# RWKV's low-rank inputs taken from the input and its difference, and attention run as one sequence of 32 units

## The chip, the cores and the metric

The kernel runs on one core of a Trainium2 chip. A core has five engines that each work through a queue of their own in order: TensorE (PE, with its weight loads as PEld), VectorE (DVE), ScalarE (ACT), GpSimd (POOL) and SyncE (SP), which here issues the weight DMAs. The metric is the time of one execution on the device in microseconds (us); lower is better.

## The reference

Four layers are computed for T = 512 positions of width D = 1024, in fp32: a convolution mixer, an RWKV-7 mixer, a gated delta rule mixer and a "stick breaking" attention, each with an MLP. The change touches two places. In the RWKV mixer, six inputs are mixed from the normed input h and its difference to the position before:

```python
xx = h_prev - h
xr, xw, xk, xv, xa, xg = h[None] + xx[None] * mu[:, None, None, :]
r, k, v = jnp.einsum('nbsd,nde->nbse', jnp.stack([xr, xk, xv]), w_rkv)
w = -jax.nn.softplus(-(w0 + jnp.tanh(xw @ w1) @ w2)) - 0.5
a = jax.nn.sigmoid(a0 + (xa @ a1) @ a2)
g = jax.nn.sigmoid(xg @ g1) @ g2
```

`w1` and `a1` are 1024x64, `g1` is 1024x160. In the attention (8 heads of 128), for each block of queries:

```python
z = jnp.einsum('bhtd,bhsd->bhts', qb, kb) * scale
ls_neg = jax.nn.log_sigmoid(-z)
log_fail = jnp.where(causal, ls_neg, 0.0)
log_rest = lax.cumsum(log_fail, axis=3, reverse=True) - log_fail
log_a = z + ls_neg + log_rest
att = jnp.where(causal, jnp.exp(log_a), 0.0)
outs.append(jnp.einsum('bhts,bhsd->bhtd', att, vb))
```

## The kernel before, in words

Activations lie transposed in SBUF, as 8 tiles (k = 0 to 7) of 128 features x 512 positions. A large matrix product is made in three parts for accuracy: the input is split into a rounded part HH (ACT, `scalar_split`, L627) and a remainder HL (DVE, L1101 here), the weights likewise into WH (ACT, L401) and WL (DVE, L409), and PE adds WH·HH, WL·HH and WH·HL (L650, L651, L656). Weights stream in as chunks through three buffers ST by SP; `plan_take`, `scalar_take` and `vector_take` place the conversion of a later chunk in the queue of an engine while an earlier one is used. A projection of 1024x1024 ("rkv" chunks 0 to 11, four for each of r, k and v) is 192 matmuls, four chunks of 48. Engines wait on counters ("tallies"); the order in each queue is the order in which the functions below write it.

**RWKV projections (us 610 to 827 of the trace).** After the rms norm, DVE scales X into TMP (L1121), ACT adds the shift and writes HT (L1074), POOL subtracts the shifted HT and writes the difference VV (L1143). TMP has two buffers. Then six mixes follow in the order W, A, G, r, k, v: DVE writes TMP = VV·mu + HT (L1107), ACT splits off HH (L627), DVE writes HL (L1101), 8 of each a mix. There is one HH and one HL, so ACT may write the next mix's HH only when the product that reads the last one has ended: that is the wait `mm.at(*free)` in `scalar_split`. The low-rank products (L1044, `tensor_lora`) are four runs of 24 matmuls: W, A, and twice G (G's 160 columns in two windows). The last ones are followed by r, k and v.

**Attention (us 2592 to 2716).** Heads 0 to 3 go together, then 4 to 7. For a head, the key blocks j = 3, 2, 1, 0 are taken in turn, each with w = 512 - 128j queries; so j = 0 is the widest. For each (head, j):

- PE "z": scores, one product of width w (L2664); ACT: ZS, abs, exp, ln, each of width w (L2704, L2707, L2709, L2711)
- DVE "softplus" (L2733, width w), "fail" and "masked" (L2736, L2737, width 128)
- PE "rest": the sums over later keys, products of width w, w - 128, ... 128 (L2674)
- DVE "log" (L2750, width w), ACT "exp" (L2718), DVE "weight" (L2753, width 128)
- PE "o": one product of width w (L2688), added up over j

These products are plain fp32, in two passes each (the trace counts x2). `ATTEND` runs four heads through six steps in turn; in one step of one head DVE does log and then, after ACT's exp, weight, and after that softplus, fail and masked of the head's next block. After the fourth block ACT writes the head's HH (L2723), DVE its HL (L2758). Then the output product "so" (192 matmuls, four chunks) begins, once HL of head 7 is written. Ahead of the loops both ACT and DVE have converted "so" chunks 0, 1 and 2.

Of the kernel before, what the change touches and what calls it, by code (L numbers as in the profile page):

```python
# [12 lines left out]
P = 128  # L13
# [26 lines left out]
def tables():  # L40
# [32 lines left out]
    "lwa": (1, 8, 128), "lg": (1, 8, 160), "rkv": (12, 8, 256), "wo": (4, 8, 256),  # L73
# [155 lines left out]
def build(nc, x, cols, tab, w, lo2, out):  # L229
    ctx = ExitStack()  # L230
    with ctx:
# [79 lines left out]
        scan_vec, gdn_vec, att_vec = tally("scan_vector"), tally("gdn_vector"), tally("att_vector")  # L311
        sumsq, scan_pool, gdn_pool = tally("squares_added"), tally("scan_pool"), tally("gdn_pool")
# [81 lines left out]
        def scalar_high(e, j):  # L394
# [3 lines left out]
            e.wait_ge(*landed(pos))  # L398
# [238 lines left out]
        def tensor_group(e, tag, n, group, k, H, L, high, low):  # L637
# [346 lines left out]
        def by4(ps, k):  # L984
# [11 lines left out]
        LORAS = ((0, 0, "W", ACT.Tanh, 0, 64), (0, 0, "A", ACT.Copy, 64, P), (1, 0, "G", ACT.Sigmoid, 0, P),  # L996
                 (1, 32, "G", ACT.Sigmoid, 96, P))
        MIXES = (("W", 1), ("A", 4), ("G", 5), ("r", 0), ("k", 2), ("v", 3))
# [6 lines left out]
        def plan_projections():  # L1005
            plan_need("rwkv", 1, 5)
            plan_rms("rwkv")
            for k in range(KT):
                tmp.use(("ht", k), half, "ht", k)
            plan_mix("W")  # L1010
            plan_take(J["lora"][0])
            big.use(("lora", 0), out_act, "lora", 0)
            plan_mix("A")
            big.use(("lora", 1), out_act, "lora", 1)
# [19 lines left out]
        def tensor_lora(e, i):  # L1034
            n, c0, mix, _, _, _ = LORAS[i]
            j = J["lora"][n]
            wh, wl = halves(j)
            ps = big.tile(("lora", i))
            e.wait_ge(*lo.at(j))
            e.wait_ge(*big.free(("lora", i)))  # L1040
            for k in range(KT):
                e.wait_ge(*norm_vec.at("mix" + mix, "lo", k))
                for part, (a, b) in enumerate(((wh, HH), (wh, HL), (wl, HH))):
# [1979 lines left out]
```

## Time and profile before

| | |
|---|---|
| time, median of 3 runs | 3138.26 us (3137.51 to 3151.96) |
| the profiled execution | 3137.9 us, of which the span is 3136.1 us |
| PE busy | 2919.8 us, 93% of the span |
| DVE, ACT, POOL busy | 1566.6, 1054.0, 185.6 us |
| chain that ended last, by engine | PE 84%, DVE 9%, ACT 5% |

An engine's busy share is a mean over a program of many stages. The two stages of the change make up some 340 us of the span, and in them PE is not always the engine that is waited for. TensorE's clock is granted in tenths of full speed (1.00 is 2.4 GHz, 0.50 is 1.2 GHz).

### The profile page before, as it was taken

How to read it: one execution, taken by the hardware profiler on the slowest of the kernel's cores; microseconds unless marked ns; L12 is line 12 of the kernel's file. 1: busy time of each engine (PE TensorE's matmuls, PEld its weight loads, DVE VectorE, ACT ScalarE, POOL GpSimd, SP SyncE). 2: the span in 40 equal slices, each digit the busy share in tenths (PEclk: the TensorE clock that was granted, in tenths of full speed). 3: DMA queues.
4: the chain of work that ended last, by engine and by line, in shares of the span. 5: the costliest groups of instructions: out<-in, count | busy, mean ns of one | idle time of the engine just before them, and what ended most of it. 6: DMA issues, size and time to landing. Idle time of an engine off the chain costs nothing.

```text
span 3136.1 us, 47827 instructions
## 1 busy us (share of the span) xinstructions
PE 2919.8 (93%) x21538; PEld 2353.9 (75%) x21538; DVE 1566.6 (50%) x2201; ACT 1054.0 (34%) x1359; POOL 185.6 (6%) x149
## 2 busy tenths in 40 slices
PE   5999999789999989999899999899999996899999
PEld 3887888657788877888666666678887874578887
DVE  6666554374477754333466666543333655343332
ACT  2225234244222325334343323232222556432221
POOL 1010000200222200000100000000000000000000
PEclk7999999989999999999999999899999998999999
DMA  7454544211000022222211111022323210122321
GB/s 268 177 193 151 189 184 148 78 67 54 15 4 3 5 108 81 96 96 104 66 66 41 41 41 41 28 83 81 113 91 104 81 54 0 54 92 71 119 85 64
DMA packets 41724, 269.66 MB, mean 86 GB/s; under 512 B 4272, under 2 KB 4528, under 8 KB 13488
## 3 DMA queue, kind: packets, MB, share of 16 engines
q1 hardware_dynamic: 39648, 260.86, 23.5%
q10 hardware_dynamic: 1872, 5.74, 0.5%
q8 instruction: 169, 2.77, 0.4%
q14 instruction: 35, 0.29, 0.0%
HBM read 264.49 MB, written 2.10 MB: 85 GB/s over the span
## 4 chain that ended last, share of the span: by engine, by line
PE 84%; DVE 9%; ACT 5%; DMA 1%; issue 1%; POOL 0%; SPq 0%; DVEq 0%; ACTq 0%
PE ps L650 21%; PE ps L651 21%; PE ps L656 21%; PE ps L2026 4%; PE ps L2780 1%; PE ps L1591 1%; PE ps L1574 1%; PE ps L1585 1%; DMA W<-w_ada 1%; PE ps L2130 1%; DVE qk L2303 1%; PE ps L2099 1%; PE ps L2156 1%; DVE v L2303 1%; PE ps L459 1%
## 5 line engine op out<-in xcount | busy, mean ns | idle before, releaser
L650 PE MATMUL ps<-HH,WH 128*128 128x512 f32 x1928 | 769.3, 399 | 40.2 <-ACT HH L627 38.8
L651 PE MATMUL ps<-HH,WL 128*128 128x512 f32 x1928 | 759.6, 394 | 0.0
L656 PE MATMUL ps<-HL,WH 128*128 128x512 f32 x1928 | 735.9, 393 | 1.7 <-DVE HL L608 1.7
L409 DVE TENSOR_TENSOR WL<-ST,WH 128x2048 fp32r<-128x2048 f32 (+3 forms) x230 | 463.2, 2015 | 243.1 <-ACT WH L401 243.1
L401 ACT ACTIVATE WH<-ST 128x2048 fp32r<-128x2048 f32 (+2 forms) x211 | 382.6, 1813 | 311.6 <-PE ps L656 295.2
L650 PEld LDWEIGHTS ps<-HH,WH 128*128 128x128 f32 x1928 | 367.7, 191 | 127.0 <-issue 48.5
L656 PEld LDWEIGHTS ps<-HL,WH 128*128 128x128 f32 x1928 | 366.6, 190 | 82.1 <-DVE HL L608 4.5
L651 PEld LDWEIGHTS ps<-HH,WL 128*128 128x128 f32 x1928 | 368.0, 191 | 78.5 <-issue 2.9
L650 PE MATMUL ps<-GH,WH 128*128 128x512 f32 x928 | 361.7, 390 | 0.0
L651 PE MATMUL ps<-GH,WL 128*128 128x512 f32 x928 | 361.1, 389 | 0.0
L656 PE MATMUL ps<-GL,WH 128*128 128x512 f32 x928 | 359.9, 389 | 0.0
L656 PEld LDWEIGHTS ps<-GL,WH 128*128 128x128 f32 x928 | 174.2, 188 | 36.4
L651 PEld LDWEIGHTS ps<-GH,WL 128*128 128x128 f32 x928 | 174.2, 188 | 36.1
L650 PEld LDWEIGHTS ps<-GH,WH 128*128 128x128 f32 x928 | 174.2, 188 | 35.7
L951 DVE TENSOR_TENSOR TMP<-TMP,ps 128x512 f32<-128x512 f32 x44 | 30.2, 687 | 239.4 <-PE ps L656 224.1
L518 POOL TENSOR_TENSOR ACC<-ACC,TMP 128x512 f32<-128x512 f32 x49 | 65.5, 1337 | 1415.2 <-ACT TMP L507 1414.5
L692 DVE SCALAR_TENSOR_TENSOR X<-ps,MOD,X 128x512 f32<-128x512 f32 x48 | 35.8, 749 | 203.9 <-PE ps L656 203.9
L880 DVE TENSOR_TENSOR GL<-TMP,GH 128x512 fp32r<-128x512 f32 x64 | 44.2, 691 | 171.2 <-ACT GH L873 171.2
L2026 PE MATMUL ps<-HH,WH 128*128 128x512 f32 x256 | 118.0, 461 | 2.9 <-ACT UU L2042 2.9
L695 DVE TENSOR_TENSOR X<-X,ps 128x512 f32<-128x512 f32 x48 | 32.8, 686 | 161.8 <-PE ps L656 161.8
L448 DVE SCALAR_TENSOR_TENSOR ADA<-ST,SM,ADA 128x512 f32<-128x512 f32 x140 | 107.8, 770 | 4.2
L943 ACT ACTIVATE GH<-TMP 128x512 fp32r<-128x512 f32 x44 | 27.8, 632 | 228.4 <-DVE TMP L951 228.4
(360 smaller groups left out, 3692.4 us busy)
## 6 DMA issues: line engine op xcount, KB each, us to landing
ST<-w_m SPq DMA_DIRECT2D x64, 1024.0 KB, 4.9
ST<-w_gu SPq DMA_DIRECT2D x44, 1024.0 KB, 4.7
ST<-w_ada SPq DMA_DIRECT2D x40, 1024.0 KB, 6.2
ST<-w_dn SPq DMA_DIRECT2D x32, 704.0 KB, 4.1
ST<-w_gin SPq DMA_DIRECT2D x16, 1024.0 KB, 4.8
ST<-w_cin SPq DMA_DIRECT2D x12, 1024.0 KB, 5.0
ST<-w_rkv SPq DMA_DIRECT2D x12, 1024.0 KB, 4.8
ST<-w_kv SPq DMA_DIRECT2D x8, 1024.0 KB, 4.7
```

The costliest lines, as they stand in the source:

```text
L401: e.activation(WH[:, j % 3, 0:n], ST[:, pos % 3, 0:n], ACT.Copy).then_inc(*hi.up(j))
L409: o = e.tensor_tensor(WL[:, j % 3, cut], ST[:, pos % 3, cut], WH[:, j % 3, cut].bitcast(F32), ALU.subtract)
L448: e.scalar_tensor_tensor(out=ADA[:, d, :], in0=tile[:, q, :], scalar=cc, in1=ADA[:, d, :], op0=ALU.mult, op1=ALU.add).then_inc(*ada.up(n, q))
L518: e.tensor_tensor(sums_of(t)[:, :], sums_of(t)[:, :], tmp.tile(("square", t, k)), ALU.add).then_inc(*sumsq.up(t, k))
L650: e.matmul(ps[:, :], wh[:, k, cs], H[:, k, :], start=(k == 0), stop=False)
L651: e.matmul(ps[:, :], wl[:, k, cs], H[:, k, :], start=False, stop=False)
L656: o = e.matmul(ps[:, :], wh[:, k, cs], L[:, k, :], start=False, stop=(k == kt - 1))
L692: e.scalar_tensor_tensor(out=X[:, m, :], in0=ps[:, :], scalar=gcol(m), in1=X[:, m, :], op0=ALU.mult, op1=ALU.add).then_inc(*res.up(tag, m))
L695: e.tensor_tensor(X[:, m, :], X[:, m, :], ps[:, :], ALU.add).then_inc(*res.up(tag, m))
L880: e.tensor_tensor(GL[:, m, :], tmp.tile((tag, m)), GH[:, m, :].bitcast(F32), ALU.subtract).then_inc(*out_vec.up(tag, m))
L2026: o = e.matmul(ps[:, :], a[:, k, c0:c0 + P], b[:, k, :], start=(k == 0 and part == 0), stop=(k == KT - 1 and part == 2))
L2303: e.scalar_tensor_tensor(out=dst[r], in0=UU[:, r, q:q + T], scalar=col("gconv", 24 * q + w0), in1=dst[r], op0=ALU.mult, op1=ALU.add).then_ ...
```

## The change

**Projections.** Since (h + d·mu) W = h W + d (mu·W), the products for w and a are now taken from h and d themselves. The chunk "lwa" holds [w1, a1] twice, 256 columns wide; DVE multiplies the second copy by mu as soon as it has landed, which is in the layer before. The mixes W and A are gone. ACT splits h (it writes HT and, right behind, HH from the same TMP), then d (HH from VV); DVE writes the remainders. One run of 48 matmuls adds all into one PSUM tile. G's two products run side by side, k by k. A new tally `input_read` (`took`) counts each HH tile as read, so that a split may overwrite tile k once the product before has read tile k for the last time. For k and v, ACT takes up that split while the projection before is at its last column block (m = 7). Some weight conversions stand elsewhere in the queues.

```diff
-    "lwa": (1, 8, 128), "lg": (1, 8, 160), "rkv": (12, 8, 256), "wo": (4, 8, 256),
+    "lwa": (1, 8, 256), "lg": (1, 8, 160), "rkv": (12, 8, 256), "wo": (4, 8, 256),
+        def vector_scale(e, pos):
+            tile = ST[:, pos % 3, :].rearrange("p (k c) -> p k c", k=KT)
...
+            for c, n, tag in ((P, 1, "W"), (P + 64, 4, "A")):
+                a = COLS["mu"][0] + 8 * n
+                part = tile[:, :, c:c + 64]
+                e.tensor_tensor(part, part, CC[:, a:a + 8][:, :, None].broadcast_to((P, KT, 64)),
+                                ALU.mult).then_inc(*scaled.up(tag))
-        def scalar_split(e, tag, bcol, free):
-            if free:
+        def read(tag, last, k):
+            return took.at(tag, k) if k < KT - 1 else mm.at(*last)
+        def scalar_split(e, tag, bcol, free, of=None):
+            if free and not of:
                 e.wait_ge(*mm.at(*free))
             for k in range(KT):
                 e.wait_ge(*norm_vec.at(tag, "t", k))
+                if of:
+                    e.wait_ge(*read(of, free, k))
...
-        def tensor_lora(e, i):
...
+        def tensor_lora(e):
...
+            for tag, c0 in (("h", 0), ("d", P)):
+                for k in range(KT):
+                    e.wait_ge(*norm_vec.at(tag, "lo", k))
+                    for part, (a, b) in enumerate(((wh, HH), (wl, HH), (wh, HL))):
+                        o = e.matmul(ps[:, :], a[:, k, c0:c0 + P], b[:, k, :],
...
+                        o.then_inc(*took.up(tag, k))
+            for k in range(KT):
+                e.wait_ge(*half.at("mixG", k))
+                for i, c0 in ((2, 0), (3, 32)):
...
+                    e.matmul(ps[:, :], wh[:, k, c0:c0 + P], HH[:, k, :], start=(k == 0), stop=False)
+                    e.matmul(ps[:, :], wl[:, k, c0:c0 + P], HH[:, k, :], start=False, stop=False)
+                e.wait_ge(*norm_vec.at("mixG", "lo", k))
...
         def scalar_projections(e):
+            scalar_take(e, ("take", J["lora"][0]))
...
             for k in range(KT):
...
                 e.activation(HT[:, k, 1:T + 1], tmp.tile(("ht", k)), ACT.Identity,
                              bias=modcol(1, 0, k)).then_inc(*half.up("ht", k))
-            scalar_split(e, "mixW", None, ("down01", 7))
-            scalar_take(e, ("take", J["lora"][0]))
+                e.activation(HH[:, k, :], tmp.tile(("ht", k)), ACT.Identity,
+                             bias=modcol(1, 0, k)).then_inc(*half.up("h", k))
+            for k in range(KT):
+                e.wait_ge(*scan_pool.at("diff", k))
+                e.wait_ge(*took.at("h", k))
+                e.activation(HH[:, k, :], VV[:, k, :], ACT.Identity).then_inc(*half.up("d", k))
+            scalar_split(e, "mixG", None, ("lora", 0), "d")
+            scalar_take(e, ("take", J["lora"][1]))
             scalar_lora(e, 0)
-            scalar_split(e, "mixA", None, ("lora", 0))
             scalar_lora(e, 1)
-            scalar_split(e, "mixG", None, ("lora", 1))
-            scalar_take(e, ("take", J["lora"][1]))
+            scalar_split(e, "mixr", None, ("lora", 3), "G")
             scalar_lora(e, 2)
             scalar_lora(e, 3)
```

DVE at the start of the projections. Before (lines 1121, 1107, 1101 as above; the six of the last row are the remaining scalings, then mix W starts):

```order
L1121 SCALAR_TENSOR_TENSOR TMP<-X,SM,RST 128x512 [waits norm_summed,norm_vector]
L1121 SCALAR_TENSOR_TENSOR TMP<-X,SM,RST 128x512
L1121 SCALAR_TENSOR_TENSOR TMP<-X,SM,RST 128x512 [waits input_high] x6
L1107 SCALAR_TENSOR_TENSOR TMP<-VV,CC,HT 128x512 [waits input_high,scan_pool] x2
L1101 TENSOR_TENSOR HL<-TMP,HH 128x512 [waits input_high]
```

And now, the same place (L1172 is the last of the eight scalings, between each two of which stands one remainder of h, L1167; L1179 is the remainder of d, L1153 and L1147 are mix G):

```order
L1172 SCALAR_TENSOR_TENSOR TMP<-X,SM,RST 128x512
L1167 TENSOR_TENSOR HL<-HT,HH 128x512 [waits input_high] x2
L1179 TENSOR_TENSOR HL<-VV,HH 128x512 [waits input_high] x8
L1153 SCALAR_TENSOR_TENSOR TMP<-VV,CC,HT 128x512 [waits scan_pool] x2
L1147 TENSOR_TENSOR HL<-TMP,HH 128x512 [waits input_high]
```

The eight remainders of h stand between the scalings, eight more of d follow, and mixes W and A (8 scalings and 8 remainders each) are gone.

ACT from the gate's split to that of r. Before (L627 splits, L401 is WH, L1067 the low-rank results):

```order
L1067 ACTIVATE ADA<-ps 64x512 [waits dense_summed]
L627 ACTIVATE HH<-TMP 128x512 [waits norm_vector] x8
L401 ACTIVATE WH<-ST 128x2048 [waits s_st1]
L1067 ACT_TABLE_LOAD
L1067 ACTIVATE ADA<-ps 128x512 [waits dense_summed]
L1067 ACTIVATE EX<-ps 32x512 [waits dense_summed]
L627 ACTIVATE HH<-TMP 128x512 [waits norm_vector] x8
```

And now (L1122 splits d; L647 G, then r; L402 is WH; L1107 the results):

```order
L1122 ACTIVATE HH<-VV 128x512 [waits input_read,scan_pool] x8
L647 ACTIVATE HH<-TMP 128x512 [waits input_read,norm_vector] x7
L647 ACTIVATE HH<-TMP 128x512 [waits dense_summed,norm_vector]
L402 ACTIVATE WH<-ST 128x2048 [waits s_st1]
L1107 ACT_TABLE_LOAD
L1107 ACTIVATE ADA<-ps 64x512 x2
L647 ACTIVATE HH<-TMP 128x512 [waits input_read,norm_vector] x7
L647 ACTIVATE HH<-TMP 128x512 [waits dense_summed,norm_vector]
L1107 ACT_TABLE_LOAD
L1107 ACTIVATE ADA<-ps 128x512
L1107 ACTIVATE EX<-ps 32x512
```

The gate's results now come behind r's split, the conversion and two results stay between the two splits, and the wait of seven of eight splits is for a tile's last reading, not for the product.

**Attention.** The 32 (head, block) pairs are numbered as units, and in step t each engine takes one part of several units. Each loop is written so (the waits are left out; they are the tallies of the same names as before):

```diff
+        ATTEND = [(h + i, j) for h in (0, 4) for j in (3, 2, 1, 0) for i in range(4)]
+        def tensor_attend(e):
+            for t in range(-1, len(ATTEND) + 3):
+                for h, j in unit(t + 1):
...
+                for h, j in unit(t - 3):
+                    e.wait_ge(*att_vec.at("weight", h, j))
...
+                for h, j in unit(t - 1):
...
+                    e.wait_ge(*att_vec.at("fail", h, j))
...
-            e.wait_ge(*att_vec.at("low", 7))
+            tensor_attend(e)
             tensor_dense(e, "so", HH, HL, attended_high, attended_low)
...
             if number["sq", 0] <= j <= number["sq", 3]:
-                stop = number["so", 2]
+                stop = number["so", 1]
```

In step t, PE does z(t+1), o(t-3), rest(t-1); ACT does the four score operations of t, exp(t-2), and HH of a finished head (t-4); DVE does log(t-2), softplus, fail and masked (t-1), weight(t-3), and HL of a finished head (t-5). DVE inside the loop before:

```order
L2750 SCALAR_TENSOR_TENSOR AT_138<-ps,ZS_134 128x384 [waits att_summed]
L2753 TENSOR_TENSOR AT_138<-AT_138,TB 128x128 [waits att_activated]
L2733 SCALAR_TENSOR_TENSOR LF_130<-ZS_134,LF_130 128x512 [waits att_activated]
L2736 TENSOR_TENSOR LF_130<-LF_130,TB 128x128 [waits att_vector]
L2737 TENSOR_TENSOR ZS_134<-ZS_134,TB 128x128
L2750 SCALAR_TENSOR_TENSOR AT_139<-ps,ZS_135 128x384 [waits att_summed]
```

And now (L2784 log, L2791 softplus, L2794 fail, L2795 masked, L2799 weight; the number behind AT, ZS and LF is the head's buffer):

```order
L2784 SCALAR_TENSOR_TENSOR AT_138<-ps,ZS_134 128x384 [waits att_vector,att_summed]
L2791 SCALAR_TENSOR_TENSOR LF_131<-ZS_135,LF_131 128x384 [waits att_activated]
L2794 TENSOR_TENSOR LF_131<-LF_131,TB 128x128 [waits att_vector]
L2795 TENSOR_TENSOR ZS_135<-ZS_135,TB 128x128
L2799 TENSOR_TENSOR AT_141<-AT_141,TB 128x128 [waits att_activated]
L2784 SCALAR_TENSOR_TENSOR AT_139<-ps,ZS_135 128x384 [waits att_vector,att_summed]
```

Log and weight of one unit no longer stand side by side: the weight behind a log is that of the unit before it. PE inside the loop before (L2664 z, L2688 o, L2674 rest):

```order
L2664 MATMUL ps<-QS,KS 128x512 [waits att_activated]
L2688 MATMUL ps<-AT_139,VT 128x256
L2674 MATMUL ps<-LF_131,TB 128x384 [waits att_vector]
L2674 MATMUL ps<-LF_131,TB 128x256
L2674 MATMUL ps<-LF_131,TB 128x128
```

And now (L2724 z, L2731 o, L2740 rest):

```order
L2724 MATMUL ps<-QS,KS 128x512 [waits att_activated]
L2731 MATMUL ps<-AT_138,VT 128x384 [waits att_vector]
L2740 MATMUL ps<-LF_132,TB 128x384
L2740 MATMUL ps<-LF_132,TB 128x256
L2740 MATMUL ps<-LF_132,TB 128x128
```

The order of the kinds is the same, but o now waits for DVE (its weight comes later in DVE's queue than the fail for which rest waits), where before rest was the one that waited. The conversion of "so" chunk 2 (WH on ACT, WL on DVE) stands behind the attention now, and the product "so" no longer waits for HL of head 7 before its first matmul, but for each tile as it comes to it.

## Rows read from the trace of the kernel before

**Rows 1.** First part of the page: busy us of the span by engine.

```profile
PE 2919.8 (93%) x21538; PEld 2353.9 (75%) x21538; DVE 1566.6 (50%) x2201; ACT 1054.0 (34%) x1359; POOL 185.6 (6%) x149
```

**Rows 2.** Windows view: width, busy us of five engines, granted clock, DMA share, GB/s.

```profile
617.00:629.00 12.00, 0.00 (x0) 0.00 (x0) 11.90 (x9) 6.27 (x10) 11.66 (x8) 0.50 0.00 1
629.00:674.00 45.00, 33.02 (x97) 20.10 (x98) 36.98 (x51) 23.16 (x32) 0.00 (x0) 0.82 0.14 47
674.00:718.00 44.00, 43.73 (x192) 35.85 (x192) 19.80 (x20) 15.62 (x19) 0.00 (x0) 1.00 0.28 96
2592.00:2607.00 15.00, 11.29 (x30) 7.75 (x31) 8.91 (x26) 8.72 (x31) 0.00 (x0) 0.50 0.00 1
2607.00:2661.00 54.00, 38.86 (x135) 22.63 (x135) 26.82 (x74) 31.61 (x74) 0.00 (x0) 0.99 0.00 0
2661.00:2669.00 8.00, 6.09 (x17) 4.13 (x17) 3.94 (x14) 4.18 (x14) 0.00 (x0) 0.59 0.00 0
```

**Rows 3.** Timeline, projections' start: start, us, engine, line, operation, idle before.

```profile
598.33 0.75 DVE L692 SCALAR_TENSOR_TENSOR X<-ps,MOD,X 128x512 f32<-128x512 f32 x1 [7.01 <-PE ps L656]
615.50 1.42 DVE L1121 SCALAR_TENSOR_TENSOR TMP<-X,SM,RST 128x512 f32<-128x512 f32 x2
617.10 7.98 DVE L1121 SCALAR_TENSOR_TENSOR TMP<-X,SM,RST 128x512 f32<-128x512 f32 x6 [0.19 <-ACT HT L1074]
617.21 11.66 POOL L1143 TENSOR_TENSOR VV<-HT 128x512 f32<-128x512 f32 x8 [7.86 <-ACT HT L1074]
617.88 0.72 ACT L1074 ACTIVATE HT<-TMP,MOD 128x512 f32<-128x512 f32 x1 [0.21 <-DVE TMP L1121]
627.89 1.52 DVE L1101 TENSOR_TENSOR HL<-TMP,HH 128x512 fp32r<-128x512 f32 x1
```

**Rows 4.** Timeline, from the gate's mix to the value projection.

```profile
664.84 1.90 ACT L401 ACTIVATE WH<-ST 128x2048 fp32r<-128x2048 f32 x1
666.75 1.28 ACT L1067 ACT_TABLE_LOAD   x1
673.14 1.15 ACT L627 ACTIVATE HH<-TMP 128x512 fp32r<-128x512 f32 x2
673.92 0.47 PE L650 MATMUL ps<-HH,WH 128*128 128x512 f32 x1 [1.42 <-ACT HH L627]
682.15 1.47 DVE L1101 TENSOR_TENSOR HL<-TMP,HH 128x512 fp32r<-128x512 f32 x2
719.03 0.47 PE L650 MATMUL ps<-HH,WH 128*128 128x512 f32 x1 [1.30 <-ACT HH L627]
764.18 0.47 PE L650 MATMUL ps<-HH,WH 128*128 128x512 f32 x1 [1.30 <-ACT HH L627]
```

**Rows 5.** Timeline, start of attention.

```profile
2592.17 2.28 DVE L409 TENSOR_TENSOR WL<-ST,WH 128x2048 fp32r<-128x2048 f32 x1
2594.49 0.28 ACT L2704 ACTIVATE ZS<-ps 128x128 f32<-128x128 f32 x1 [2.32 <-DVE WL L409]
```

**Rows 6.** Timeline, inside attention, and its end.

```profile
2629.82 0.69 DVE L2733 SCALAR_TENSOR_TENSOR LF<-ZS,LF 128x512 f32<-128x512 f32 x1 [2.00 <-ACT LF L2711]
2630.54 0.29 DVE L2736 TENSOR_TENSOR LF<-LF,TB 128x128 f32<-128x128 f32 x1
2630.95 0.55 DVE L2750 SCALAR_TENSOR_TENSOR AT<-ps,ZS 128x384 f32<-128x384 f32 x1
2634.38 0.69 DVE L2733 SCALAR_TENSOR_TENSOR LF<-ZS,LF 128x512 f32<-128x512 f32 x1 [2.00 <-ACT LF L2711]
2645.40 2.42 PE L2674 MATMUL ps<-LF,TB 128*128 128x512 f32 x8 [1.63 <-DVE AT L2750]
2650.47 3.60 PE L2688 MATMUL ps<-AT,VT 128*128 128x512 f32 x8
2651.33 0.19 PEld L2688 LDWEIGHTS ps<-AT,VT 128*128 128x128 f32 x1 [0.24 <-issue]
2715.59 0.50 PE L650 MATMUL ps<-HH,WH 128*128 128x512 f32 x1 [1.41 <-DVE HL L2758]
```

More of the change, by code:

```diff
@@ L1085, in scalar_projections @@
             pre = scalar_pre(e, 0)
-            for tag, before in (("r", ("lora", 3)), ("k", ("r", 7)), ("v", ("k", 7))):
-                scalar_split(e, "mix" + tag, None, before)
+            for tag, then in (("r", "k"), ("k", "v"), ("v", None)):
                 for n, j in enumerate(J[tag]):
@@ L1090, in scalar_projections @@
                     for m in (2 * n, 2 * n + 1):
+                        if m == 7 and then:
+                            scalar_split(e, "mix" + then, None, (tag, 7), tag)
                         e.wait_ge(*mm.at(tag, m))
@@ L1118, in vector_projections, with low @@
             e.wait_ge(*norm_vec.at("rwkv", "rstd"))
+            def low(k):
+                e.wait_ge(*half.at("h", k))
+                e.tensor_tensor(HL[:, k, :], HT[:, k, 1:T + 1], HH[:, k, :].bitcast(F32),
+                                ALU.subtract).then_inc(*norm_vec.up("h", "lo", k))
             for k in range(KT):
@@ L1122, in vector_projections @@
                                        in1=RST[:, :], op0=ALU.mult, op1=ALU.mult).then_inc(*norm_vec.up("ht", k))
-            vector_mix(e, "W", 1)
+                if k:
+                    low(k - 1)
+            low(KT - 1)
+            for k in range(KT):
+                e.wait_ge(*half.at("d", k))
+                e.tensor_tensor(HL[:, k, :], VV[:, k, :], HH[:, k, :].bitcast(F32),
+                                ALU.subtract).then_inc(*norm_vec.up("d", "lo", k))
+            vector_mix(e, "G", 5)
             vector_take(e, ("take", J["lora"][0]))
-            vector_mix(e, "A", 4)
-            vector_mix(e, "G", 5)
-            vector_take(e, ("take", J["lora"][1]))
             pre = vector_pre(e, 0)
@@ new lines, in vector_attend @@
+        def vector_attend(e):
+            for t in range(len(ATTEND) + 5):
+                for h, j in unit(t - 2):
+                    w_ = T - P * j
+                    e.wait_ge(*att_mm.at("rest", h, j))
+                    e.wait_ge(*att_vec.at("masked", h, j))
+                    if j < 3:
+                        e.wait_ge(*att_mm.at("o", h, j + 1))
+                    elif h > 3:
+                        e.wait_ge(*att_mm.at("o", h - 4, 0))
+                    e.scalar_tensor_tensor(out=ATT[h % 4][:, 0:w_], in0=rest_b.tile(("rest", h, j))[:, 0:w_],
+                                           scalar=-1.0, in1=ZST[h % 4][:, 0:w_], op0=ALU.mult,
+                                           op1=ALU.add).then_inc(*att_vec.up("log", h, j))
+                for h, j in unit(t - 1):
+                    w_ = T - P * j
+                    L, Z = LFT[h % 4][:, OFF[j]:OFF[j] + w_], ZST[h % 4][:, 0:w_]
+                    e.wait_ge(*att_act.at("ln", h, j))
+                    e.scalar_tensor_tensor(out=L, in0=Z, scalar=0.0, in1=L, op0=ALU.max,
+                                           op1=ALU.add).then_inc(*att_vec.up("softplus", h, j))
+                    e.wait_ge(*att_vec.at("softplus", h, j))
+                    e.tensor_tensor(L[:, 0:P], L[:, 0:P], tb("sup"), ALU.mult).then_inc(*att_vec.up("fail", h, j))
+                    e.tensor_tensor(Z[:, 0:P], Z[:, 0:P], tb("sup"), ALU.mult).then_inc(*att_vec.up("masked", h, j))
+                for h, j in unit(t - 3):
+                    Aw = ATT[h % 4][:, 0:P]
+                    e.wait_ge(*att_act.at("exp", h, j))
+                    e.tensor_tensor(Aw, Aw, tb("sup"), ALU.mult).then_inc(*att_vec.up("weight", h, j))
+                for h, j in unit(t - 5):
+                    if j == 0:
+                        e.wait_ge(*att_act.at("high", h))
+                        e.tensor_tensor(HL[:, h, :], out_b.tile(("o", h))[:, :], HH[:, h, :].bitcast(F32),
+                                        ALU.subtract).then_inc(*att_vec.up("low", h))
```

244 lines of the change are left out of this document (103 added, 141 removed).

## The prediction

> **What bounds the kernel now.** I read the page first: PE is busy 93% of the span [rows 1], so time can only come from stretches in which PE waits or runs at half clock. The windows view shows two such stretches at the places of the change. From 617 to 629 PE does nothing while DVE and POOL are busy all the time; from 629 to 674 it is busy 33.0 of 45 us, at a mean clock of 0.82, for 97 matmuls; then it runs full, 43.73 of 44 us for 192 matmuls at clock 1.00 [rows 2]. 96 low-rank matmuls at that pace (43.73 / 192 = 0.228 us) are 21.9 us, but the stretch takes 57. In attention PE seems busy too (38.9 of 54 us), yet DVE and ACT are at 26.8 and 31.6 [rows 2], so no engine is full and the order of the waits counts.
>
> The timeline tells who is waited for. At the projections' start two scalings run by themselves, 1.42 us for both, 0.71 each; the next six take 7.98 beside POOL's differences, 8 of them in 11.66, 1.46 each [rows 3]. So beside POOL a two-input DVE operation comes every 1.45 us; I read that as 0.71 of its own and 0.74 in which POOL holds it up. A remainder in the last of POOL's time takes 1.52 [rows 3]. After the mixes, r starts at 673.92, k at 719.03, v at 764.18, each after PE idled for ACT's HH: 1.42, 1.30, 1.30 [rows 4]. In attention, softplus waits 2.00 us for ACT's ln, which comes once exp and the score operations of that head are through: 4.56 us from one softplus to the next (2629.82 to 2634.38) [rows 6].
>
> **The projections, part by part.** The number of low-rank matmuls stays 96 (48 for h and d, 48 for G). What changes is when their inputs are there.
>
> *Start.* The first scaled tile is at about 616.2, then ACT writes HT and HH, 0.72 each with 0.1 of overlap and the hand-off of 0.2 [rows 3]: HH(0) at 617.7. Remainder 0 then ends near 618.7 (0.3 still held by POOL, 0.7 of its own). Thirteen two-input operations of DVE follow until remainder 7 (scalings 3 to 7 and remainders, in pairs), 13 x 0.71 = 9.2, and POOL's seven further differences hold it up for 7 x 0.74 = 5.2. That is 633.1. The eight remainders of d follow at 0.71, with 0.4 for the hand-over: 639.2. Mix G: 0.72 for its first scaling, then 8 pairs. The time from the first HH to the last HL of such a mix is 10.48 (673.14 to 682.15 + 1.47 = 683.62) [rows 4], together 11.2: 650.4.
>
> *G to r.* ACT has HH(7) of G at 649.7. It then does WH and a table load, 664.84 to 668.05 = 3.2 [rows 4], and two low-rank results (about 0.55 each, as HH: 1.15 for two [rows 4]), ready to write r's HH(0) from 652.9 + 1.1 = 654.0. PE follows 0.78 later, as 673.92 does after 673.14 [rows 4]: r starts at 654.7, 19.2 earlier. PE must be done with G by then: G's 48 matmuls are 10.9 us at full clock against the 11.2 of the mix, so they end just behind the remainders, 651.1. At half clock (0.50 until 629 [rows 2]) h and d would drag on to about 644, and G would end up to 3 us behind 654.7; I leave this for the range.
>
> *r.* Its first chunk is 48 x 0.228 = 10.9 long, to 665.7. Chunk 1 needs WL, which stands behind r's remainders on DVE now: those end at 654.0 + 10.48 = 664.4, plus WL 2.28 [rows 5] is 666.7: PE stalls 1.0. Left: 18.2.
>
> *k and v.* Their splits are taken up before the product ends. The 1.30 of idle goes at each, and the first matmuls no longer follow ACT and DVE at their pace: from 719.03 to 764.18 are 45.15 us for 192 matmuls, of which 43.7 is PE's own work [rows 2, 4]; so 1.5 each, 3.0 together. The projections give 18.2 + 3.0 = **21.2**.
>
> *The price of POOL's company.* If the new remainders fit beside POOL as nearly free, the start is paced at 1.45 per k; h ends about 5.3 earlier: 26.5. If each of the fourteen operations costs 1.45, 16.3. The rows lie between, since POOL's work is only 8 differences long [rows 3]. The Trainium skill, GPSIMD Engine Reference, Specifications, says that the two engines share their SBUF interfaces and collide on DVE instructions with two SBUF inputs. That speaks against the change, which puts eight more such operations there; the rows' 0.71 against 1.45 agree with it. Without that rule I would take 26.5; the sum stays with the rows.
>
> *Costed at nothing.* The scaling of the doubled chunk (two products of 128 x 512 elements, 0.7 to 1.5 us each) and the longer conversion lie in the layer before, where DVE stood idle for 7.01 us ahead of one residual [rows 3]; without that cover they cost 1 to 4 us. WH moved ahead of HT (1.90 [rows 4]) falls under the wait for the norm; if not, 1.9.
>
> **Attention.** What goes: WL of "so" chunk 2, 2.28 us on DVE, after which the first score operation had waited 2.32 [rows 5]. DVE is free at 2592.3. ACT's own WH goes too.
>
> The new order makes a ring: PE's rest(t-1) ends, DVE does log, softplus, fail, masked, weight, PE does o (which waits for that weight) and rest(t) behind it, and only then can DVE take the next log. The cost of a turn, for j = 0 (width 512): log 0.69 - 0.08 (a following independent operation starts 0.08 early: fail and masked, 0.29 each, take 0.41 from 2630.54 to 2630.95), softplus 0.72 (2629.82 to 2630.54), 0.41, weight 0.29, hand-off 0.06: 2.09 [rows 6]. PE: a pass of 512 takes 0.43 (load 0.19 + 0.24 [rows 6]; 3.60 for eight agrees), so o is 0.86 and rest, 1280 columns in two passes, 2.15 (2.42 with its start [rows 6]). Hand-off PE to DVE 0.26, an estimate over the 0.19 and 0.21 of [rows 3]. Sum 5.36. With widths 384, 256, 128 (log and softplus 0.55, 0.42 between the two, 0.29): 1.82 + 1.93 + 0.26 = 4.01; 1.56 + 1.08 + 0.26 = 2.90; 1.29 + 0.43 + 0.26 = 1.98. Four blocks 14.25, eight heads **114.0**. ACT needs about 3.2 of the 5.36 and hides; z lies under DVE's part. Fill and drain I take as even, within 1.5 either way. At full clock PE is free at 2706.3.
>
> The ring contains PE's passes, so it feels the clock. At half clock a head costs 6.44 more (the PE parts of the four turns: 3.01 + 1.93 + 1.08 + 0.43). Before, the clock was 0.50 from 2592 to 2607, 0.99 to 2661, 0.59 to 2669 [rows 2]. I take the same two stretches: 15 us hold four narrow units and 1.4 of width 256, 1.7 + 1.5 = 3.2; the other about 1.4. The end is 2710.9. The product "so" then starts at once, where it had waited 1.41 for the last HL and began at 2715.59 [rows 6]: **4.7** saved. With no half clock it would be 9.3. The Trainium skill, TensorE: Matmul & The Clock Gate, HAM oscillation, ties the fall of the clock to PE standing idle. In the new ring PE is never idle for more than a turn of DVE, about 2.1 us; by that page alone I would take the 9.3. The row at 0.59 with PE busy 6.09 of 8 us [rows 2] shows that it falls without a long idle; the measurement decides.
>
> Chunk 2 of "so" is converted after the attention. It lands about 5 us after 2711, and with 2.28 behind it is ready near 2719, while chunks 0 and 1 keep PE until 2711 + 21.8 = 2733. Hidden; cost nothing.
>
> **Sum.** 3137.9 (the profiled execution, 0.4 below the median of 3138.26) - 21.2 - 4.7 = **3112.0**.
>
> **Rivals.**
> 1. *The pipeline overlaps as its name says.* If o did not hold up rest, PE alone would bound it: z, o and rest are 6.44 + 2.15 = 8.6 for the four widths, and ACT would take over at the narrow ones, so about 9.6; 77 us for eight heads: 2670, so 39 to 41 us less: about 3073. The order of PE's queue speaks against it: o stands ahead of rest. Chance 0.05.
> 2. *The clock falls and stays down (slower).* PE waits more evenly in the ring than before: its share (z, o and rest over a turn) is 3.87 / 5.36 = 0.72 at width 512, and 0.64, 0.52 and 0.32 for the others. If it stays at half clock through attention, eight heads cost 51.5 more than at full clock, 46.9 more than my sum: 3158.9. It decides once attention loses 26 us more than forecast. For it: 0.50 to 2607 at the narrow units; against it: 0.99 over 54 us. Chance 0.06.
> 3. *Further dips,* at the narrow units in the middle and in the low-rank products: 5 to 14 us more, 3117 to 3126. Chance 0.15.
> 4. *Full collision* with POOL, 16.3 instead of 21.2: 3117. Chance 0.10.
> 5. *No collision,* 26.5: 3107. Chance 0.10.
>
> The forecast has 0.54.
>
> **How the numbers follow.** The bounds 16.3 and 26.5, and 9.3 or further dips in attention, give 3102 to 3126. This leaves out rivals 1 and 2 and the tails. A measurement of this kernel tells about 0.5% from no change, 15.7 us. Faster than that means below 3122.6: the forecast, rivals 1, 4, 5 and about a quarter of 3, less a little for what I overlook: 0.83. Same: the rest of 3 and a forecast that is 10 too good, 0.11. Slower: 0.06, rival 2.
>
> **What would show it.** Projections: h's last remainder at 633 (628 or 638 by the bounds); first matmul of r near 654.7; a stall of about 1 us before r's second chunk, for WL; no idle over 0.3 at k and v. Attention: the turn of width 512 at 5.36, DVE's log waiting for rest and PE's o for the weight, PE and DVE busy by turns; end at 2711 less the 21 of before. The prediction is wrong if the turn is under 4 (then PE runs ahead), if the windows show clock 0.50 over more than 40 us of attention, or if r's start is held by PE's own backlog in G.

## The result and the profile after

| | before | after |
|---|---|---|
| median of 8 runs | 3145.24 us (3137.51 to 3151.96) | 3127.01 us (3121.47 to 3129.66) |
| the profiled execution, its span | 3137.9, 3136.1 us | 3128.1, 3126.3 us |

The ratio is 0.9939, with a 95% interval of 0.9926 to 0.9952: faster by 18 us, where 26 were forecast, and at 3127.0 a microsecond outside the range of 3102 to 3126. Five more runs of the kernel before moved its median from the 3138.26 shown ahead of the prediction to 3145.24.

The first part of the page of the changed kernel (busy us by engine):

```profile
PE 2929.2 (94%) x21538; PEld 2364.3 (76%) x21538; DVE 1552.8 (50%) x2187; ACT 1054.3 (34%) x1359; POOL 184.4 (6%) x149
```

And its windows view (columns as in [rows 2]):

```profile
617.00:629.00 12.00, 9.18 (x17) 4.99 (x18) 11.59 (x13) 7.51 (x13) 7.73 (x7) 0.50 0.00 0
629.00:640.00 11.00, 10.54 (x32) 7.62 (x31) 10.75 (x16) 7.08 (x13) 1.99 (x2) 0.67 0.00 1
640.00:650.00 10.00, 10.00 (x45) 8.07 (x44) 9.48 (x12) 5.93 (x7) 0.00 (x0) 1.00 0.00 0
668.00:700.00 32.00, 32.00 (x143) 26.50 (x142) 14.86 (x16) 11.11 (x14) 0.00 (x0) 1.00 0.38 136
```

PE has the same 21538 matmuls and is busy 9.4 us longer: a sign, not a proof, that more of them ran at half clock. In the projections PE works from 617 on, where it had done nothing until 629 [rows 2]. The timeline of the stage (start, us, engine, line, operation, idle before):

```profile
614.37 1.42 DVE L1172 SCALAR_TENSOR_TENSOR TMP<-X,SM,RST 128x512 f32<-128x512 f32 x2
616.53 1.08 DVE L1167 TENSOR_TENSOR HL<-HT,HH 128x512 fp32r<-128x512 f32 x1 [0.74 <-ACT HH L1117]
617.54 1.52 DVE L1172 SCALAR_TENSOR_TENSOR TMP<-X,SM,RST 128x512 f32<-128x512 f32 x1
618.98 0.68 DVE L1167 TENSOR_TENSOR HL<-HT,HH 128x512 fp32r<-128x512 f32 x1
...
628.78 2.76 DVE L1167 TENSOR_TENSOR HL<-HT,HH 128x512 fp32r<-128x512 f32 x2
631.46 4.89 DVE L1179 TENSOR_TENSOR HL<-VV,HH 128x512 fp32r<-128x512 f32 x8
...
652.34 0.47 PE L670 MATMUL ps<-HH,WH 128*128 128x512 f32 x1 [1.02 <-ACT HH L647]
664.30 0.50 PE L670 MATMUL ps<-HH,WH 128*128 128x512 f32 x1 [0.82 <-DVE WL L410]
```

All here is 1.13 us earlier than before, as the first scaling shows (614.37 against 615.50 [rows 3]). h's last remainder ends 17.2 us after that start (631.54), r begins 38.0 after it, and its second chunk waits 0.82 for WL. The waits of PE from r to the end of v, by what it waited for (us in total, times, longest), first before, then after:

```profile
PE ps L650 <- ACT HH L627: 4.0, 3, 1.4
```

```profile
PE ps L670 <- ACT HH L647: 1.0, 1, 1.0
PE ps L670 <- DVE WL L410: 0.8, 1, 0.8
```

Of three waits for HH one is left: k and v start without one. In attention, the timeline of the changed kernel at full clock, then with part of a turn at half clock (lines 2784 log, 2799 weight, 2731 o, 2740 rest, 2724 z):

```profile
2628.83 0.69 DVE L2784 SCALAR_TENSOR_TENSOR AT<-ps,ZS 128x512 f32<-128x512 f32 x1 [3.16 <-PE ps L2740]
2630.57 0.28 DVE L2799 TENSOR_TENSOR AT<-AT,TB 128x128 f32<-128x128 f32 x1
2630.91 1.13 PE L2731 MATMUL ps<-AT,VT 128*128 128x512 f32 x2 [1.89 <-DVE AT L2799]
2631.87 2.32 PE L2740 MATMUL ps<-LF,TB 128*128 128x512 f32 x8
2634.03 0.39 PE L2724 MATMUL ps<-QS,KS 128*128 128x128 f32 x2
2634.22 0.69 DVE L2784 SCALAR_TENSOR_TENSOR AT<-ps,ZS 128x512 f32<-128x512 f32 x1 [3.37 <-PE ps L2740]
...
2688.14 0.69 DVE L2784 SCALAR_TENSOR_TENSOR AT<-ps,ZS 128x512 f32<-128x512 f32 x1 [3.16 <-PE ps L2740]
2695.23 0.69 DVE L2784 SCALAR_TENSOR_TENSOR AT<-ps,ZS 128x512 f32<-128x512 f32 x1 [5.07 <-PE ps L2740]
...
2704.69 0.79 PE L670 MATMUL ps<-HH,WH 128*128 128x512 f32 x1
```

The reader sees the ring: DVE waits 3.37 us for rest, PE waits 1.89 for the weight at the end of DVE's step, and one turn is 5.39 us (2628.83 to 2634.22). With part of the turn at half clock it is 7.09 (2688.14 to 2695.23), and the windows view has a mean granted clock of 0.73 there:

```profile
2690.00:2700.00 10.00, 7.67 (x14) 3.75 (x15) 2.15 (x6) 1.11 (x2) 0.00 (x0) 0.73 0.00 0
```

The product so follows without a wait, 121.2 us after DVE's first softplus. In the kernel before, this took 119.9 (2595.65 to 2715.59 [rows 6]). The two first softplus, before and after:

```profile
2595.65 0.29 DVE L2733 SCALAR_TENSOR_TENSOR LF<-ZS,LF 128x128 f32<-128x128 f32 x1 [1.19 <-ACT LF L2711]
```

```profile
2583.50 0.28 DVE L2791 SCALAR_TENSOR_TENSOR LF<-ZS,LF 128x128 f32<-128x128 f32 x1
```

So in these traces the new loop by itself is 1.2 us slower than the old one; what attention gains, it gains ahead of the first softplus (see the conversion alone, below).

**Stage by stage.** The same operations of GpSimd and the ends of the span cut each trace into stages: its memset of HT (projections begin), its first TT of an RWKV head (they end), and its last addition of squares ahead of attention and the first behind it (attention, with the products q and so around it). What is left is code that the change does not touch. The table has all traces of this study, stages in us, and all timed runs of each kernel.

| kernel | projections | attention | the rest | runs: mean (lowest to highest), number |
|---|---|---|---|---|
| before, first trace | 209.9 | 309.4 | 2616.8 | 3145.0 (3135.1 to 3155.0), 64 |
| before again | 209.6 | 309.5 | 2628.5 | among these |
| projections only | 187.4 | 309.5 | 2631.4 | 3126.8 (3122.0 to 3130.0), 6 |
| attention only | 209.7 | 307.5 | 2625.3 | 3146.7 (3134.8 to 3153.4), 12 |
| conversion only | 209.7 | 308.4 | 2621.9 | 3141.7, 1 |
| after, first trace | 187.4 | 307.4 | 2631.6 | 3125.5 (3117.0 to 3130.0), 14 |
| after again | 187.3 | 307.4 | 2620.5 | among these |
| splits wait for the end | 189.5 | 308.2 | 2627.7 | 3127.3, 1 |
| differences on VectorE | 186.0 | 307.3 | 2625.6 | 3120.7, 1 |
| five added matmuls | 188.5 | 308.2 | 2615.9 | 3123.4 (3114.4 to 3133.4), 6 |
| ten added matmuls | 189.6 | 307.4 | 2631.2 | 3128.7 (3125.2 to 3131.7), 5 |
| rest first | 187.4 | 275.9 | 2630.2 | 3095.3, 1 |
| log last | 187.4 | 265.1 | 2629.8 | 3082.6 (3077.2 to 3085.8), 5 |
| log last, differences on VectorE | 186.4 | 265.7 | 2623.8 | 3080.5 (3077.7 to 3082.6), 5 |

With the same code the projections repeat within 0.3 us; attention repeats within 0.1 as it was before, and lies between 307.3 and 308.2 as changed. They gave 22.4 and 2.0, though in two of the later traces attention gave only 1.2. The code that nobody touched varies by 15.7. Between the two first traces it took 14.8 us more, which is why their spans differ by only 9.8, where the two stages alone differ by 24.6.

### The profile page after: what moved, and what is told of

The parts are those of the page before. It is cut to its first block, busy times and chain, and to the rows that moved or that the text cites. A ratio compares the mean times of both kernels' runs of the same rounds, so it can differ in the third digit from the quotient of the medians.

```text
span 3126.3 us, 47881 instructions
## 1 busy us (share of the span) xinstructions
PE 2929.2 (94%) x21538; PEld 2364.3 (76%) x21538; DVE 1552.8 (50%) x2187; ACT 1054.3 (34%) x1359; POOL 184.4 (6%) x149
## 4 chain that ended last, share of the span: by engine, by line
PE 86%; DVE 9%; ACT 4%; DMA 1%; issue 1%; POOL 0%; SPq 0%; DVEq 0%; ACTq 0%
PE ps L670 21%; PE ps L671 21%; PE ps L676 21%; PE ps L2083 4%; PE ps L2825 1%; PE ps L2740 1%; PE ps L1631 1%; PE ps L1648 1%; PE ps L1642 1%; PE ps L2731 1%; PE ps L2187 1%; DMA W<-w_ada 1%; PE ps L2156 1%; DVE qk L2360 1%; DVE v L2360 1%
## 5 line engine op out<-in xcount | busy, mean ns | idle before, releaser
L402 ACT ACTIVATE WH<-ST 128x2048 fp32r<-128x2048 f32 (+1 forms) x211 | 383.5, 1818 | 319.0 <-PE ps L676 290.3
```

The source lines that it names most:

```text
L402: e.activation(WH[:, j % 3, 0:n], ST[:, pos % 3, 0:n], ACT.Copy).then_inc(*hi.up(j))
```

## The experiments

**Each half alone.** `projections only` has all of the diff up to the attention, `attention only` the rest.

> Only the RWKV projections are changed, attention is as before. Theory A (the stage's saving is as measured in the trace of after, and the rest of the difference is the clock elsewhere): the stage from the rms norm to the first of RWKV's heads is 22.6 us shorter than before; in the delta rule stage, whose code is the same, the clock dips vary by run; the median lies 15 to 23 us under that of before. Theory B (a start some 22 us earlier puts the delta rule stage onto clock dips each time): the delta rule stage is 13 us longer than before in this run too, and the median is only about 9 us under before.

> Only the attention is changed. The delta rule stage stands where it stands before, so by theory B it has no dips of 0.50 in its heads and takes as long as in the profile of before; by theory A it may have them or not. Attention: ring turns of 5.2 to 5.4 us at width 512 at full clock and 7.1 at half, the product so starts 2 to 10 us earlier relative to the last norm of q than before, according to how many wide units fall at half clock. Median 0 to 5 us under before by theory A.

> The kernel before, unchanged, for a second trace. Theory A: the delta rule stage is longer than in the first trace by up to 14 us, with the granted clock at 0.93 to 0.97 in 50 us windows that showed 1.00, since this kernel's times reach from 3137.5 to 3152.0; theory B: the clock is 1.00 in these windows again and the time is within 3 us of 3137.9. Ratio to before 1.00.

> The changed kernel, unchanged, for a second trace. Theory A: stage times of projections and attention as in the first trace within 2 us (attention within 6, by the clock), the delta rule stage different by several us. Theory B: the delta rule stage again 13 us longer than in the first trace of before. Ratio to before 0.993 to 0.995.

Measured: projections only, ratio 0.9940 (0.9923 to 0.9956); attention only, 1.0010 (0.9995 to 1.0025); before again, 0.9989 (0.9977 to 1.0001); after again, 0.9933 (0.9914 to 0.9951). The attention's 2 us show in the stage alone: the median of attention only is 3 us above that of before, where 0 to 5 under it were expected. The delta rule stage of the kernel before was 10 us longer in its second trace with the same code. Its heads begin at these additions on GpSimd (the timeline, first and last, of the first trace of before, the second one, and the first of after):

```profile
1602.19 1.28 POOL L2415 TENSOR_TENSOR e<-u,TG 128x512 f32<-128x512 f32 x1 [53.96 <-DVE GC L2277]
...
1961.07 1.27 POOL L2415 TENSOR_TENSOR e<-u,TG 128x512 f32<-128x512 f32 x1 [47.63 <-DVE GC L2277]
```

```profile
1600.13 1.28 POOL L2415 TENSOR_TENSOR e<-u,TG 128x512 f32<-128x512 f32 x1 [53.96 <-DVE GC L2277]
...
1969.08 1.27 POOL L2415 TENSOR_TENSOR e<-u,TG 128x512 f32<-128x512 f32 x1 [47.62 <-DVE GC L2277]
```

```profile
1580.12 1.28 POOL L2472 TENSOR_TENSOR e<-u,TG 128x512 f32<-128x512 f32 x1 [53.96 <-DVE GC L2334]
...
1951.73 1.27 POOL L2472 TENSOR_TENSOR e<-u,TG 128x512 f32<-128x512 f32 x1 [47.40 <-DVE GC L2334]
```

They are 358.9, 369.0 and 371.6 us apart. The windows view at the same place of one head, first trace of before, then first of after, then second of after, tells why:

```profile
1687.50:1697.50 10.00, 9.64 (x47) 6.16 (x46) 7.79 (x16) 4.59 (x8) 0.00 (x0) 1.00 0.00 0
1697.50:1703.50 6.00, 6.00 (x43) 4.49 (x44) 2.82 (x10) 3.21 (x5) 1.27 (x1) 1.00 0.01 3
```

```profile
1668.00:1678.00 10.00, 9.62 (x44) 6.15 (x44) 7.70 (x16) 4.59 (x8) 0.00 (x0) 0.97 0.00 0
1678.00:1684.00 6.00, 6.00 (x30) 4.95 (x30) 0.71 (x5) 3.05 (x5) 0.00 (x0) 0.50 0.01 3
```

```profile
1664.00:1674.00 10.00, 9.64 (x46) 6.14 (x46) 7.80 (x16) 4.58 (x8) 0.00 (x0) 1.00 0.00 0
1674.00:1680.00 6.00, 6.00 (x44) 4.49 (x44) 2.81 (x10) 3.25 (x5) 1.27 (x1) 1.00 0.01 3
```

The same instructions, as dense as in the other trace, and once the granted clock is 1.00, once 0.50: 43 or 44 matmuls in 6 us, or 30. The last two pairs are of one and the same program. As the heads repeat, the dip can return: of the seven steps from head to head, one has it in the first trace of before (54.2 us instead of 51.1), two in the second of after, and most in the first of after. So theory B as I had put it (13 us more each time) falls: in the second trace of after the first and the last of these additions are 361.8 us apart, in that of before 369.0. Theory A stands for what a single trace shows.

**The ring.** If log stands last in VectorE's step, rest of the next unit no longer waits behind it:

```diff
 def vector_attend(e):
     for t in range(len(ATTEND) + 5):
-        for h, j in unit(t - 2):   # log
...
         for h, j in unit(t - 1):   # softplus, fail, masked
...
         for h, j in unit(t - 3):   # weight
...
+        for h, j in unit(t - 2):   # log
...
```

> All of the change, but VectorE's step in attention is softplus, fail, masked (t-1), weight (t-3), then log (t-2). Theory ring (one turn holds all of VectorE's step and TensorE's o and rest, since log stands ahead of everything and o ahead of rest): with log last, rest(t-1) runs under the next step, the ring is open, and a turn is what the busiest engine needs: 3.9 us at width 512 (TensorE), 2.6, 1.6 and 1.4 for the others, 9.5 a head, 76 us in all against 114. The attention stretch (last square-sum addition on GpSimd ahead of it to the first behind it) falls from 307.4 to 268 to 275 us. Rival (the turn is set by the engines' hand-offs and ScalarE's four operations, not by this order): stretch within 5 us of 307.4.

Measured: ratio 0.9789 (0.9771 to 0.9807), attention 265.1 us, 42.2 less than after and 3 under the 268 to 275 expected. The timeline at width 512 (L2780 softplus, L2797 log, lines of PE as above):

```profile
2610.42 0.69 DVE L2797 SCALAR_TENSOR_TENSOR AT<-ps,ZS 128x512 f32<-128x512 f32 x1 [1.56 <-PE ps L2740]
2611.03 0.68 DVE L2780 SCALAR_TENSOR_TENSOR LF<-ZS,LF 128x512 f32<-128x512 f32 x1
2611.08 0.81 PE L2731 MATMUL ps<-AT,VT 128*128 128x384 f32 x2
2611.73 2.32 PE L2740 MATMUL ps<-LF,TB 128*128 128x512 f32 x8
2613.88 0.39 PE L2724 MATMUL ps<-QS,KS 128*128 128x128 f32 x2
2614.08 0.69 DVE L2797 SCALAR_TENSOR_TENSOR AT<-ps,ZS 128x512 f32<-128x512 f32 x1 [1.64 <-PE ps L2740]
```

The turn shown is 3.66 us, PE goes from o to rest to z without a gap, and only DVE waits. The windows view shows PE full at the wide units and, past the start, the clock full too:

```profile
2583.00:2588.00 5.00, 4.54 (x15) 3.56 (x16) 3.89 (x17) 4.68 (x19) 0.00 (x0) 0.50 0.00 0
2610.00:2620.00 10.00, 10.00 (x37) 5.94 (x36) 5.61 (x15) 6.50 (x17) 0.00 (x0) 1.00 0.00 1
2650.00:2660.00 10.00, 10.00 (x33) 5.42 (x31) 5.25 (x14) 4.66 (x9) 0.00 (x0) 1.00 0.00 0
```

The other way to open the ring is on TensorE: rest (t-1) ahead of o (t-3).

```diff
 def tensor_attend(e):
-                for h, j in unit(t - 3):   # o
...
                 for h, j in unit(t - 1):   # rest
...
+                for h, j in unit(t - 3):   # o
```

> All of the change, but TensorE's step in attention is z, rest (t-1), then o (t-3). Theory ring: rest no longer stands behind o, which waits for weight; the ring is then rest, log, softplus, fail: 2.15 + 0.26 + 0.61 + 0.72 + 0.29 + 0.06 = 4.1 us at width 512, 2.95, 2.0 and 1.5 for the others, 84 us for eight heads instead of 114; stretch 277 to 285 us. Rival (the order on TensorE is not what costs, since weight comes only 0.3 us behind masked): stretch within 5 us of 307.4.

Measured: attention 275.9 us, a microsecond under the range expected. The turn is 4.13 us, where the sum over the shorter ring gave 4.1:

```profile
2618.80 0.69 DVE L2784 SCALAR_TENSOR_TENSOR AT<-ps,ZS 128x512 f32<-128x512 f32 x1 [2.11 <-PE ps L2733]
2622.93 0.69 DVE L2784 SCALAR_TENSOR_TENSOR AT<-ps,ZS 128x512 f32<-128x512 f32 x1 [2.11 <-PE ps L2733]
```

**The tally of reads.**

```diff
                         if m == 7 and then:
-                            scalar_split(e, "mix" + then, None, (tag, 7), tag)
+                            scalar_split(e, "mix" + then, None, (tag, 7))
```

> All of the change, but the splits of k and v wait for the end of the product before, as they did before the change. My sum gave the tally of reads 1.5 us at each of k and v: the projections' stage grows from 187.35 to 190.3 us, with 1.3 us of idle ahead of each product. Rival (the gain lies in the earlier start of r alone, the slower pace at a product's start would be there anyway): 188.7 or less.

Measured: 189.5, so 2.2 for both, between the two (one trace). The wait came back, but as 0.81 and not 1.30, because ACT now stands ready at the product's end and no longer behind its last copy:

```profile
699.45 0.47 PE L670 MATMUL ps<-HH,WH 128*128 128x512 f32 x1 [0.81 <-ACT HH L647]
```

**GpSimd's company.** The eight differences are written by VectorE (in `vector_projections`, one behind each remainder of h) and leave `pool_projections`.

```diff
                 if k:
                     low(k - 1)
+                    diff(k - 1)
             low(KT - 1)
+            diff(KT - 1)
...
```

> All of the change, but VectorE takes the eight differences (each behind the remainder of h of the tile), GpSimd none. Theory collision (each of GpSimd's differences holds VectorE up by 0.74 us): VectorE's sixteen scalings and remainders lose the 5.8 us of hold-up and gain 8 x 0.71 = 5.7: first scaling to last remainder of h is 17.2 us again, within 1, and each operation takes 0.7 us. Rival (the operations are slow for another reason, such as waits for ScalarE): 17.2 + 5.7 = 22.9 us.

```profile
613.98 1.42 DVE L1178 SCALAR_TENSOR_TENSOR TMP<-X,SM,RST 128x512 f32<-128x512 f32 x2
616.13 0.69 DVE L1173 TENSOR_TENSOR HL<-HT,HH 128x512 fp32r<-128x512 f32 x1 [0.74 <-ACT HH L1117]
616.74 0.68 DVE L1168 TENSOR_TENSOR VV<-HT 128x512 f32<-128x512 f32 x1
617.35 0.74 DVE L1178 SCALAR_TENSOR_TENSOR TMP<-X,SM,RST 128x512 f32<-128x512 f32 x1
...
628.82 0.69 DVE L1173 TENSOR_TENSOR HL<-HT,HH 128x512 fp32r<-128x512 f32 x1 [0.20 <-ACT HH L1117]
```

Every operation takes 0.68 to 0.74, where beside GpSimd some took 1.08 to 1.52. VectorE has eight operations more and is done 15.5 us after its start instead of 17.2, which is also less than the sum had; the stage is 1.4 us shorter (0.9 in the next run, with log last). The hold-up is GpSimd's. The Trainium skill, GPSIMD Engine Reference, Specifications, names this case (VectorE instructions with two SBUF inputs), and the trace agrees: 0.68 against 1.52.

**Both.** Log last and the differences on VectorE together.

> The change with log last in VectorE's step of attention and the eight differences of h on VectorE instead of GpSimd. If the two are independent, the stages take what they took alone: projections 186.0 us, attention stretch 265.1; median 1 to 2 us under the 3084 of log last. Rival (the differences' order moves later stages onto more or fewer clock dips, which is worth more than 1.4 us): up to 6 us to either side.

Measured: ratio 0.9798 (0.9784 to 0.9811), beside 0.9789 of log last alone: no difference that can be told. It is as good as log last, and both beat the two kernels of this case, by 2% and 1.4%.

**Where the later stages start.** In the product for v (n is the chunk), matmuls whose result is overwritten:

```diff
+            if tag == "v" and n == 2 and k == 0 and group[0] == first:
+                for _ in range(5):
+                    e.matmul(big.tile((tag, first))[:, :], wh[:, 0, 0:P], H[:, 0, :], start=True, stop=True)
```

> The changed kernel with five added matmuls (results overwritten) in the middle of the product for v, 1.15 us of work on TensorE. Theory A (where the later stages start does not matter on average): median 1 us above the changed kernel's 3127, and projections 188.5. Theory C (the time of the unchanged stages depends on when they start, because the clock's dips there fall otherwise): median away from 3128 by 3 us or more, and the stages outside projections and attention, 2620 to 2632 us in the traces of the new projections, shift by as much.

> As the last, with ten added matmuls, 2.3 us. Theory A: median 2 us above 3127, projections 189.7. Theory C: away from 3129 by 3 us or more.

Measured: 0.9932 (0.9912 to 0.9952) and 0.9949 (0.9936 to 0.9961). The stage grew by 1.1 and 2.3 us as it should, but a kernel with more work had the shortest rest of all with the new projections (2615.9 us), and the fastest run of those that also have the attention of the change (3114.4), with 359.0 between those two additions, as in the first trace of before. Its runs spread over 19 us, so the means (3123.4, 3128.7, and 3125.5 without additions) decide nothing between theories A and C. Against a fixed tie to the start speaks that the first of these additions stood at 1579.27 here and at 1579.70 with log last, and the seven steps took 359.0 and 371.9.

**The conversion alone.** The kernel before with "so" chunk 2 converted behind the attention:

```diff
             if number["sq", 0] <= j <= number["sq", 3]:
-                stop = number["so", 2]
+                stop = number["so", 1]
...
```

> The kernel before, with one part of the change: the conversion of chunk 2 of the product so behind the attention, loops and projections as before. My sum gave 4.7 us to attention: 2.3 of it is the conversion's time on VectorE, the rest the ring against the old loop at the clock of the first trace. Theory D (the ring gives nothing, the conversion all): the attention stretch falls from 309.4 to 307.1 us, as much as the whole change to attention measured (307.4). Rival (the ring has its share): 308.5 or more.

Measured: 308.4 in one trace. The conversion gives 1.0, and the rest of the change to attention another 1.0 in most traces (307.3 to 307.5) and little in the two at 308.2. Neither theory is right. The score operation had waited 2.32 for the conversion [rows 5]; now it waits for TensorE's first score, which follows the last norm of q, as the timeline shows:

```profile
2596.05 0.69 DVE L2630 TENSOR_TENSOR QS<-QS,SQ 128x512 f32<-128x512 f32 x1
2597.70 0.28 ACT L2704 ACTIVATE ZS<-ps 128x128 f32<-128x128 f32 x1 [2.86 <-PE ps L2664]
```

It starts 0.96 after that norm's end, where before it was 2.24 (2591.56 + 0.69 to 2594.49): 1.3 saved of 2.3. The change also lets each score wait for its own head's norm, and in it the first score operation stands at 2581.94, before the last norm's end at 2583.6. From the last addition of squares to the first softplus the change takes 3.6 us less than before (172.8 for 176.4); its loop then takes 1.2 more (121.2 for 119.9, and 120.0 in this run), and the product up to the first addition 0.3 more. So the 2.0 us come from the earlier start, and the staggered loop, with the half clock that fell into it, gave nothing.

## Why the prediction was right and wrong

**Projections: right, 22.4 for 21.2.** Counted from the first scaling, h's last remainder came after 17.2 us (17.6 by the sum), r after 38.0 (39.2), and the stall for WL was 0.82 (1.0). Of the 1.2 us at r, 0.4 lie in h and 1.3 in d's remainders, and mix G took 0.4 more than its sum. The eight remainders of d took 4.89, 0.61 each, where I had put 0.71 and 0.4 for the hand-over; independent operations of VectorE overlap by 0.08, which I had used in attention and not here. Within its stage r came 20.4 us earlier, so the boundaries gave 2.8 by what is left (22.4 - 20.4 + 0.8), and 2.2 by the run that undid them, for 3.0. The price of GpSimd's company was rightly taken between the bounds: 17.2 us lie half way between the 12.5 and 22.5 of the 628 and 638 in the prediction. Half clock while h and d ran did not hold r up, though PE had no idle time in G (10.00 of 10 us from 640 on): it ended G at 651.3 and still waited 1.02 for r's HH. What was costed at nothing cost nothing that can be seen: the memset of HT stands at 608.0 to 609.2 in the traces with the old projections and at 607.6 to 609.8 in those with the new, and with chunk 2 converted behind attention PE is busy 24.00 of the 24 us from 2704 to 2728.

**Attention: mechanism right, term mis-sized, 2.0 for 4.7.** The ring turned at 5.18 to 5.39, 4.05, 2.93 and 2.02 us where the sum had 5.36, 4.01, 2.90 and 1.98, and the two runs that opened it settle the cause. From the first softplus to the product, 121.2 us were measured for the 118.6 of the sum (114.0 and 4.6 for the half clock). Two terms make up the 2.6. The half clock was put together wrongly: "the other about 1.4" was 5.2, as three of the eight wide turns took 7.1 us, 1.7 more each, and the 3.2 for the start was 0.8, in the narrow turns there; together 6.0 for 4.6. I had placed the dips where they had been before. The fill and drain, taken as even, cost 1.2 with what the changes of width do to single turns, within the 1.5 that I had allowed. What the sum never did was to set the new loop beside the old one: a wide turn was 4.56 us before (2629.82 to 2634.38 [rows 6]) and 5.36 by the sum, so that the stagger could pay only where four heads end and the next four begin (12.2 us from one softplus to the next before, 2643.53 to 2655.75). Rival 1 named what was not done: the pipeline does not overlap, because log leads VectorE's step and o leads rest; done so, it gave 42 us, against the 39 to 41 of that rival.

**The total: the wrong step is the base.** The prediction took "3137.9 (the profiled execution, 0.4 below the median of 3138.26)" and let the rest of the program stand as it was in that trace. The kernel's runs reach from 3135.1 to 3155.0, with a mean of 3145.0, and that trace has the shortest rest of the four with the old projections. With the stages' 24.4 less, a mean of 3120.6 would have been due. Measured are 3125.5 over 14 runs, 19.4 under before's mean. So of the 13.5 us between this mean and the 3112.0 of the forecast, 7.1 are the base, 2.7 the attention (4.7 put, 2.0 measured), 1.2 come off for the projections, and 4.9 stay open. With the base at the mean, the forecast would have been 3119.1. Luck has a part in the stages too: in attention too much half clock at the start hid part of what was missing at the wide units, and what the projections gave beyond the sum hid part of what attention lacked.

**What stays open.** Some 5 us of the gain are not in the means. Projections only has them too (3126.8, where 3122.6 were due), and attention only, 1.7 above before's mean, shows no gain. The rest of the program took 2616.8 to 2628.5 us in four traces of the old projections (mean 2623.1) and 2615.9 to 2631.6 in ten of the new (mean 2626.8). That the shift of the start moves the later stages onto more dips on average is possible; the delayed kernels did not show it, nor exclude it. Whether the place of the dips is drawn anew at each start or depends on when a stage begins was not settled.

## What to carry to other kernels

When a loop is staggered over units, write down what each engine does in one step in order, and follow each wait into the next step: an operation that finishes the old unit (here log) ahead of the one that starts the new one (softplus) closes a ring through all engines, and the stagger buys nothing (here the loop was 1.2 us slower than the old one); moving one block of lines was worth 42 us. Compare stages between the same operations of two traces, not spans, when the clock dips at will. And take the spread of the base from more than three runs before a forecast of under 1%.

## What the hardware showed that I had not expected

The granted clock falls to 0.50 with PE busy 9.6 of the 10 us ahead of it, and at the same place of the same program in one execution and not in another (the windows of the delta rule heads, first and second trace of after), worth 3 us a head and up to 13 us in eight. The Trainium skill, TensorE: Matmul & The Clock Gate, Part 1, says that the point at which the clock rises at the start of matmul work varies from run to run of one kernel, and calls the cost of this ramp under 1% of a typical span. The dips here are falls inside dense work, of which that passage does not speak; they come to 0.4%, as much as the effects under study. In attention the clock was at 1.00 past the start with log last, PE busy 10.00 of 10 us at the wide units and 7.58 of 10 from 2620 to 2630, and also with rest first, PE busy 8.2 to 9.9 of 10; in the ring of the change it fell in three of eight wide turns. That the fuller engine kept the clock up is likely from these, but no run was made to show it.
